# Seven block products in the last quarter of each MLP of a two-layer trunk, with sums made by adding DMAs

## The reference, cut to what matters

```python
def squared_relu_mlp(h, w_up, w_down):      # h 512x1024, w_up 1024x4096, w_down 4096x1024
    a = jax.nn.relu(h @ w_up)
    return (a * a) @ w_down

x = x + rmsnorm(mix, g[1])
hn = rmsnorm(x, g[2])
x = x + rmsnorm(squared_relu_mlp(hn, w_mlp_up[layer], w_mlp_down[layer]), g[3])
```

## Time and profile before

| | us |
|---|---|
| three runs | 1074.98, 1075.75, 1076.94 |
| median | 1075.75 |
| the profiled execution, its own time | 1075.44 |
| its span in the trace | 1073.6 |
| PE busy in it | 1056.8 (98%) |
| DVE, ACT, POOL busy | 748.7 (70%), 538.6 (50%), 189.3 (18%) |

### The profile page before, as it was taken

The page is one execution under the profiler, slowest core; times in us unless marked ns, Lnnn a source line. Parts: engine busy times, 40 slices in busy tenths (PEclk is TensorE's granted clock), DMA queues, the critical chain, the costliest instruction groups (busy, mean ns, idle before and its releaser), DMA issues.

```text
span 1073.6 us, 14865 instructions
## 1 busy us (share of the span) xinstructions
PE 1056.8 (98%) x5408; PEld 859.5 (80%) x5408; DVE 748.7 (70%) x1286; ACT 538.6 (50%) x1016; POOL 189.3 (18%) x333
## 2 busy tenths in 40 slices
PE   9999999999999999999999999999999999999997
PEld 8877779888888888888778766679888888888886
DVE  5455636596697696687589898526596696696685
ACT  6677645253453453425554567745254443453422
POOL 0464320000000000005413387520000000000005
PEclk9999999999999999999999999999999999999999
DMA  9531505544535445422613333006553535535402
GB/s 301 115 79 41 118 1 133 123 100 97 115 82 118 105 92 118 96 62 53 140 36 79 79 79 80 1 1 144 112 111 86 118 79 118 115 82 118 106 12 79
DMA packets 52009, 99.94 MB, mean 93 GB/s; under 512 B 4704, under 2 KB 4832, under 8 KB 51936
## 3 DMA queue, kind: packets, MB, share of 16 engines
q1 hardware_dynamic: 51216, 98.61, 40.4%
q10 hardware_dynamic: 720, 0.38, 0.1%
HBM read 96.88 MB, written 2.10 MB: 92 GB/s over the span
## 4 chain that ended last, share of the span: by engine, by line
PE 91%; DVE 5%; issue 1%; ACT 1%; DMA 1%; POOL 0%; DVEq 0%; POOLq 0%; SPq 0%; ACTq 0%
PE bank L2062 11%; PE bank L2060 11%; PE bank L2061 11%; PE bank L2437 7%; PE bank L2435 7%; PE bank L2436 7%; PE bank L2070 6%; PE bank L2072 6%; PE bank L2071 6%; PE bank L2219 3%; PE bank L2461 2%; PE bank L2460 2%; PE bank L2459 2%; PE bank L2288 2%; PE bank L2274 2%
## 5 line engine op out<-in xcount | busy, mean ns | idle before, releaser
L2060 PE MATMUL bank<-r_hi,w_hi 128*128 128x512 f32 (+1 forms) x456 | 177.5, 389 | 0.0
L2061 PE MATMUL bank<-r_hi,w_lo 128*128 128x512 f32 (+1 forms) x456 | 177.4, 389 | 0.0
L2062 PE MATMUL bank<-r_lo,w_hi 128*128 128x512 f32 (+1 forms) x456 | 177.4, 389 | 0.0
L1651 DVE TENSOR_TENSOR w_lo<-w_raw,w_hi 128x1024 fp32r<-128x1024 f32 x84 | 102.0, 1222 | 70.9 <-ACT w_hi L1170 70.7
L1170 ACT ACTIVATE w_hi<-w_raw 128x1024 fp32r<-128x1024 f32 x84 | 88.0, 1056 | 119.4 <-PE bank L2062 82.9
L2435 PE MATMUL bank<-w_hi,hid_hi 128*128 128x512 f32 x336 | 130.7, 389 | 0.0
L2436 PE MATMUL bank<-w_lo,hid_hi 128*128 128x512 f32 x336 | 130.7, 389 | 0.0
L2437 PE MATMUL bank<-w_hi,hid_lo 128*128 128x512 f32 x336 | 130.7, 389 | 0.0
L1179 ACT ACTIVATE w_hi<-w_raw,gT 128x512 fp32r<-128x512 f32 x96 | 64.5, 716 | 106.6 <-DMA w_raw<-in_w_mlp_up 75.1
L814 POOL TENSOR_TENSOR acc<-acc,G 128x512 f32<-128x512 f32 x8 | 13.0, 1651 | 594.3 <-ACT waste L1026 594.3
L2062 PEld LDWEIGHTS bank<-r_lo,w_hi 128*128 128x128 f32 (+1 forms) x456 | 85.2, 187 | 18.2
(11 more groups left out here) (215 smaller groups left out, 2149.4 us busy)
## 6 DMA issues: line engine op xcount, KB each, us to landing
w_raw<-in_w_mlp_up SPq DMA_DIRECT2D x64, 512.0 KB, 6.4
w_raw<-in_w_mlp_down SPq DMA_DIRECT2D x64, 512.0 KB, 6.9
w_raw<-in_b_w_in SPq DMA_DIRECT2D x16, 512.0 KB, 6.8
w_raw<-in_a_w_in SPq DMA_DIRECT2D x8, 512.0 KB, 9.3
w_raw<-in_a_w_out SPq DMA_DIRECT2D x8, 512.0 KB, 5.8
w_raw<-in_b_w_out SPq DMA_DIRECT2D x8, 512.0 KB, 6.0
xt<-in_x_turned SPq DMA_DIRECT2D x8, 256.0 KB, 4.9
X<-in_x SPq DMA_DIRECT2D x4, 512.0 KB, 11.1
```

Of the source, the lines that this page charges most:

```text
L1651: nc.vector.tensor_tensor(half_of(w_lo[:, u % 2, :], a), b_of(PRODUCTS[i][1], a), half_of(w_hi[:, u % 2, :], a).bitcast(f32), ALU.subtract ...
L2060: nc.tensor.matmul(bank, whi, xhi, start=start, stop=False)
L2061: nc.tensor.matmul(bank, wlo, xhi, start=False, stop=False)
L2062: return nc.tensor.matmul(bank, whi, xlo, start=False, stop=stop)
```

## The change

The last quarter gets the seven products too, in both layers (168 matmuls in place of 192). `down`, `hid_high`, `hid_low`, `totals`, `weight_sum` and `t3_sum` go. What was made by DVE in the weights is made by adding DMAs issued from GpSimd: a block is added by the DMA engines to what lies in its place, from HBM or from SBUF. So are most sums of accumulators. Signs of S1, S3 and S4 are turned so that all weight sums are additions. In each quarter part 4 now follows up 3.

```diff
-A_PLACE = (0, 1, 2, 3, 0, 1, 2)
+def a_place(q, i):
+    return (PARTS * q + i) % 4
-PHASE = (... ("part", 3), ("part", 4), ("up", 3), ("part", 5), ("part", 6))
+PHASE = (... ("part", 3), ("up", 3), ("part", 4), ("part", 5), ("part", 6))
+LAST_BANKS = (2, 0, 4, 0, 2, 4, 2)
+COPIED = (5, 4, 6)
+Y_ORDER = ((0, 1), (1, 1), (0, 0), (1, 0), (2, 1), (3, 1), (2, 0), (3, 0))
```

GpSimd (new):

```diff
+            def added(place, src, done):
+                dst = raw(place).rearrange("p (k n) -> p k n", k=4)
+                for a in range(2):
+                    rows = slice(64 * a, 64 * a + 64)
+                    nc.gpsimd.dma_start(dst[rows], src[rows], accum_op=ALU.add).then_inc(done, 16)
+            def weight_sums(layer, q):                       # quarters 0 to 2
+                pool.wait_ge(b_lo_done, part_no(layer, q, 0, 1))
+                added(b_place(q, "T1"), down_block(layer, q, "B12"), t_made)
+                pool.wait_ge(b_lo_done, part_no(layer, q, 1, 1))
+                added(b_place(q, "T2"), down_block(layer, q, "B22"), t_made)
+                weight_t3(layer, q)
+                weight_t4(layer, q)
+            def acc_sum(layer, into, term, times):           # 512 KB, SBUF to SBUF
+                if times:
+                    pool.wait_ge(*added_to(layer, into, times))
+                nc.gpsimd.dma_start(acc[:, into], acc[:, term], accum_op=ALU.add).then_inc(acc_added[into], 16)
+            def last_sums(layer):
+                weight_t1(layer)
+                pool.wait_ge(part_out, out_no(layer, LAST - 1, 2, 1))
+                acc_sum(layer, 2, 0, 0)
+                pool.wait_ge(part_out, out_no(layer, LAST - 1, 3, 1))
+                acc_sum(layer, 3, 1, 0)
+                weight_t2(layer)
+                pool.wait_ge(part_out, out_no(layer, LAST - 1, 4, 1))
+                pool.wait_ge(*added_to(layer, 2, 1))
+                acc_sum(layer, 0, 4, 0)
+                pool.wait_ge(part_out, out_no(layer, LAST - 1, 6, 1))
+                pool.wait_ge(acc_v, 3 * layer + 3)
+                acc_sum(layer, 2, 6, 1)
+                weight_t3(layer, LAST)
+                pool.wait_ge(term_out, 6 * layer + 2)
+                for into, times in ((3, 1), (1, 0), (0, 1)):
+                    acc_sum(layer, into, COPIED[0], times)
+                weight_t4(layer, LAST)
+                acc_sum(layer, 2, COPIED[0], 2)
+                pool.wait_ge(mixed_out, 2 * layer + 2)
+                acc_sum(layer, 3, COPIED[1], 2)
+                acc_sum(layer, 1, COPIED[1], 1)
+                pool.wait_ge(term_out, 6 * layer + 6)
+                acc_sum(layer, 2, COPIED[2], 3)
```

ACT and DVE in the last quarter. `copied` moves products 0, 1 (negated) and 2 from PSUM to an accumulator place; `mixed` adds product 2 to product 1's copy; `total` is one of three remaining subtractions; `last_term` adds products 3 to 6 to the totals:

```diff
+                a_highs(LAST, 1) ... b_highs(LAST, 2)        # ACT
+                copied(layer, 0)
+                a_highs(LAST, 3) ; b_highs(LAST, 3)
+                copied(layer, 1)
+                a_highs(LAST, 4)
+                # layer 0: copied(2) here; layer 1: behind b_highs(4) and a_highs(5)
...
+                b_lows(LAST, 1)                              # DVE
+                for n in range(3):
+                    total(layer, n)
+                S2 ; a_lows(2) ; b_lows(2) ; S4 ; a_lows(3) ; b_lows(3)
+                mixed(layer)
+                a_lows(4) ; b_lows(4) ; a_lows(5) ; b_lows(5) ; a_lows(6)
+                last_term(layer, 3)
+                b_low(layer, LAST, 6, 0)
+                last_term(layer, 4)
+                # layer 1
+                last_term(layer, 5, (0,), 1) ; last_term(layer, 5, (0,)) ; mean_square(norm, 0)
+                b_low(layer, LAST, 6, 1)
+                last_term(layer, 5, (1,), 1) ; mean_square(norm, 1) ; last_term(layer, 5, (1,))
+                x_update(norm, 0) ; last_term(layer, 6, (0,)) ; x_update(norm, 1) ; mean_square(norm, 2)
+                last_term(layer, 6, (1,)) ; x_update(norm, 2, (1,)) ; last_gained() ; mean_square(norm, 3)
+                x_update(norm, 2, (0,)) ; x_update(norm, 3, (1,)) ; x_update(norm, 3, (0,))
+                # layer 0
+                b_low(layer, LAST, 6, 1) ; mean_square(norm, 0) ; mean_square(norm, 1)
+                last_term(5, (0,), 1) ; last_term(5, (0,)) ; last_term(5, (1,), 1) ; last_term(5, (1,))
+                x_update(norm, 0) ; x_update(norm, 1) ; split(U["qi"], (0,)) ; last_term(6, (0,))
+                low(2, 0) ; split(U["qi"], (1,)) ; split(U["qi"], (2,)) ; split(U["qi"], (3,))
+                mean_square(norm, 2) ; low(2, 1) ; last_term(6, (1,)) ; x_update(norm, 2)
+                split(U["qi"] + 1, (0,)) ... split(U["qi"] + 1, (3,))
+                mean_square(norm, 3) ; low(2, 2) ; x_update(norm, 3) ; split(U["ki"]) ; low(2, 3)
```

More of the change, by code:

```diff
@@ L969, in split @@
                     act.wait_ge(*w_spent(w_before(u)))
-                if name[:3] == "out" or name[:3] == "mlp" and mlp_role(layer, u)[0] == "down":
+                    if u == U["qi"] + 1:
+                        act.wait_ge(b_lo_done, part_no(0, LAST, 6, 1))
+                if name[:3] == "out":
                     last = nc.scalar.activation(w_h, whole, ACT.Copy)
@@ L1090, in attention, with highs @@
                 norm = 2 * layer + 1
+                def highs(n, place):
+                    for u, half in HIGHS[layer].get((n, place), ()):
+                        if half is None:
+                            split(u)
+                        else:
+                            split_half(u, half)
                 for n in range(-1, 17):
@@ L1135, in attention @@
                                 y_square(norm, j, c)
-                    for u in SPLITS[layer].get(n, ()) if n >= 0 else ():
-                        if u not in HALVED and u not in COPIES_FIRST:
-                            split(u)
+                    highs(n, 2)
                 o_high(layer, 7)
@@ L1370, in _ @@
             high(3, 3)
[L1371 to L1372 removed]
+            split(70)
+            split(71)
             mlp(1)
[L1374 to L1375 removed]
         @block.vector
@@ L1515, in attention, with lows @@
                 pending = []
+                def lows(n, place):
+                    for u, half in LOWS[layer].get((n, place), ()):
+                        if half is None or u == SHARED:
+                            split(u)
+                        else:
+                            split_half(u, half)
                 for n in range(-1, 17):
@@ L1559, in attention @@
                     pending = []
-                    for u in SPLITS[layer].get(n, ()) if n >= 0 else ():
-                        if u not in POOL_UNITS and u not in NEXT_SLOT:
-                            split(u)
+                    lows(n, 3)
                     others(n, 2)
```

793 lines of the change are left out of this document (412 added, 381 removed), and 3 rows, old and new, of the table HIGHS.

## The result

| | before | after |
|---|---|---|
| median | 1075.95 us (4 runs) | 1126.17 us (4 runs, 1120.78 to 1132.05) |
| profiled execution, its own time | 1075.44 | 1123.98 |
| its span | 1073.6 | 1122.2 |

The ratio is 1.0466, 95% interval 1.0434 to 1.0499: the change makes the kernel 50 us slower. My forecast was 1071.5 with a range from 1064.5 to 1088. It was wrong in sign and size.

The account below looks back on a forecast made before the run. PE's matmuls were taken to bound the MLPs, with DVE likely to take over in the last quarters. Layer 1's 3.5 plus layer 0's 0.4 us made 3.9 off 1075.44: 1071.5 us, range 1064.5 to 1088.

Parts of the forecast that it names:

- PE's step and count: Last quarters: 192 matmuls become 168 at 0.2267 us, 5.44 us a layer, 10.9 in all if PE sets the pace.
- Quarters 0 to 2: Both layers: DVE's removed weight sums gain 0, replacements arrive in time; cost 0, up to 1 us a quarter if cover is thinner.
- A costly issue: Sign of being wrong: a GpSimd issue costs so much that twelve between T0 + 7 and T0 + 24 set the pace.
- The adds in the last quarter: 5 MB before accumulator 3 take 21.4 us at the loads' pace against 20.1 available; about 0.3 us, taken as in time.
- rival B: Last quarters: adds late, last_term 3 holds DVE, PE waits before product 6; 1092, chance 0.27 with milder forms from 1078 up.
- The far bound: Last quarters: an add moves its bytes twice, 7.0 us per MB, 39 us; 15 to 20 us a layer, 1110.
- the indexer's loads: Layer 0's last quarter: two 1 MB loads share the DMA engines, up to 2 x 4.9 us more, half in the way.
- Layer 1's end: After product 6 in layer 1: end at T0 + 44.3 where it was T0 + 47.8, giving 3.5 us.
- layer 0's: Layer 0's end: DVE's list brings qi_work to near T0 + 43.5, before T0 + 45.3; 0.4 of 5.4 us is left.
- one or two such would take 1 us: Layer 1's end: an update beside a GpSimd gain takes 1.79 in place of 0.75 us; one or two take 1 us.
- the list of 31.9 us of DVE work: Layer 1's last quarter: DVE's work up to product 6's last needed split, wanted at T0 + 34.0, so DVE just keeps up.
- DVE "near 90%": Expected sign in the last quarters: DVE busy near 90%, PE idle 0.3 us before product 2 and 3 us before qi_work.

Follow-up runs that it names:

- e2: The changed kernel with the eleven accumulator sums of each layer moving one partition of 128, every issue and wait kept: 1092.89 us (1.0156).
- e3: The changed kernel with the four weight sums of each layer's last quarter moving one partition of 64 per transfer, waits kept: 1085.87 us (1.0094).
- e7: The changed kernel with all adds of the last quarters, weight and accumulator sums, cut to one partition each, issues and waits kept: 1086.19 us (1.0089).
- e9: The changed kernel with weight adds and the sync engine's weight loads (not the attention output's) split by columns over 128 partitions: 1102.25 us (1.0243).
- e14: The changed kernel with GpSimd's descriptor ring at 4096 bytes in place of 2048, room made by bf16 unused squares: 1114.86 us (1.0374).
- e6: A kernel of DMAs alone, the phases of e5 with GpSimd's ring at 16384 bytes in place of 2048: eight adds from HBM over 64 partitions 25.9 us.
- e15: e9 with layer 0's loads for the next layer issued only after the first half of product 6's weights is split: 1097.11 us (1.0196).
- e12: e9 with the bytes of all adds of the last quarters left out, one partition each, issues and waits kept: 1077.22 us (1.0009).
- e16: e12 with GpSimd's multiplications by the gain in the norms after the MLPs cut to 8 columns of 512: 1069.64 us (0.9938).
- e4: The changed kernel with each layer's eleven accumulator sums made as GpSimd additions in place of adding DMAs, nothing left out: 1123.13 us (1.0450).
- e10: The kernel before the change with the sync engine's weight loads over 128 partitions, as in e9: 1075.56 us (0.9992).
- e5: A kernel of DMAs alone, GpSimd's ring at 2048 bytes, comparing forms of loads and adds: eight adds from HBM over 64 partitions 33.0 us.

## Why the prediction was wrong

- **PE's step and count: right.** 24 matmuls fewer a layer at 0.2267 us.
- **Quarters 0 to 2, "cost 0": wrong by 4.3 us** (1.7 and 2.6), though inside the "up to 1 us a quarter" that the sum left out. Where a row shows an idle time, PE waits for the split of T2 or for DVE's squares (L1785), which stand behind it in DVE's list. I allowed T1 twice a load's 7.35 us and gave T2 "more", but in every quarter GpSimd stood 7.3 to 10.9 us at the ring between the two halves of T2, which no row of before could show. In layer 0 only quarter 0 lost time by it (1.7 us), with the halt from 230.1 to 239.9:

```profile
239.93 3.09 POOL L878 DMA_DIRECT2D w_raw<-in_w_mlp_down  x3 [9.81 <-issue]
```

  A costly issue was among my signs of being wrong, a halt was not. The loss is not steady: e2, e3 and e7, with the same adds there, lost 4.4, 5.8 and 6.9 us. With wide transfers (e9), or with the larger ring (e14, both stretches 244.80 us), the cost is the 0 that I had said.
- **The adds in the last quarter, "just in time": the step that failed.** I took 5 MB x 3.5 + 3.9 = 21.4 us. Between T0 and accumulator 3 in layer 1 GpSimd's queue moved 7.27 million bytes (6.9 MB) in 90.8% of 43.9 us: 5.75 us per MB. Both factors were short. The bytes, because T2 and one accumulator sum, issued 2 and 1 us ahead of T0, were still to be moved then (and part of the sum behind accumulator 3 came along). The pace, because I took it from the start's loads at 301 GB/s (3.2 us per MB, had I divided by their 93% as I did by the 48% of rival B), most of which go over 128 partitions, for weight adds that go over 64 and sums that took 1.8 times a copy (e6). The adds also began late, T3 at T0 + 12.8 and 14.7. The far bound of 7.0 us per MB was there; its 39 us, counted from T0 + 7.1, end at T0 + 46, between the T0 + 43.9 and T0 + 50.7 measured. I chose the near end, though what the prediction cites from the Trainium skill, Collectives: The Full Stack, spoke for the far one.
- **Rival B was the right mechanism** (`last_term` 3 holds DVE, the split of product 6's weights behind it, PE idle before product 6), and the indexer's loads do add in layer 0: 4.8 us by e15, where I had 5. Its chance of 0.27 and its price, 1092, were too low; its far bound, 15 to 20 us a layer, is near what came: PE stood 17.7 and 9.3 us before product 6, and the stretches lost 25.0 and 15.6 by the table. Even its 1110 was short of 1126.
- **Layer 1's end, "gives 3.5", and layer 0's, "0.4": both mis-sized.** With no byte to wait for (e12) layer 1 gives 0.6 and layer 0 loses 1.7 up to `qi_work` and 1.0 behind it. The term is the update beside a GpSimd gain, "one or two such would take 1 us": four in layer 1 cost 4, and two in layer 0, with the small products, 4.2. With them at 0.75 (e16) `qi_work` comes at T0 + 42.8 and the end gives 4.4, beside my T0 + 43.5 and 3.5. So the list of 31.9 us of DVE work holds as far as these ends can show; what I missed is that it pushed the updates under GpSimd's products.
- **DVE "near 90%", PE idle 0.3 us before product 2:** DVE was busy 51 to 59%, since it waited for adds itself; PE idled 3.2 us there, and T2 was the cause, not DVE.

Left open: the first 2.4 us of the change, before any MLP. e2, e3, e7 and e4, with the same program there, have 0.6, 0.2, 0.3 and 4.5; I take it for the spread of a start full of loads, but that is argued. No version beat the kernel before; e10, a tie, is the nearest. e16 is faster only because it leaves work out.

## What to carry to other kernels

Before work goes to DMA because "the engines are 6% busy", sum all bytes of the stretch, those still queued at its start too, and price them by transfers of the same partitions, piece size and operation; measure an unseen kind alone, with one and with eight in flight, before building on it. GpSimd's descriptor ring is a resource of its own. And when a list gets tight, look at what its instructions will now run beside: a DVE operation on two SBUF operands beside GpSimd cost 1.0 us more in each update here, and up to GpSimd's whole row in e4.

## What was not expected of the hardware

- Loads of 512 KB over 128 partitions: eight in 13.4 us; over 64: 22.1 us (e5).
- With a ring of 2048 bytes GpSimd halts for 6.7 and 9.5 us after two or three adds (e5); the same kernel took 1158.2, 1126.2 and 1114.9 us with 1024, 2048 and 4096.
- An add inside SBUF takes 1.8 times a copy (22.9, 12.5 us), an add from HBM 1.15 times a load by the same queue (25.9, 22.4), both in e6.
- Two 128x512 subtractions of DVE took 10.79 us beside GpSimd's additions, 1.28 without (e4).
